# Reordering VectorE work in one retention loop and one mixer block, and rebuilding a small embedding stage, in a fused three-layer forward pass on Trainium2

## The reference, cut to what matters

```python
# first block
z   = rms_norm(x, norm1_g) @ w_in            # 18 column tiles of 128
mix = concat([gmlp(z_a), rglru(z_b), hgrn2(z_c), pool(z_d)])
x   = x + mix @ w_out
hf  = causal_dwconv(rms_norm(x, norm2_g) @ w_up)       # 2 x 2816
x   = x + (gelu(gt) * val) @ w_down
gate = sigmoid(rms_norm(x, norm3_g) @ w_pg)            # 1024 x 1024
x   = x + (p @ w_pe) * gate                            # p: 512 x 256, w_pe: 256 x 1024
x   = rms_norm(x, final_g)

# hgrn2: gated linear recurrence, 4 heads, chunks of 64;
# within a chunk the pairwise decays exp(b_t - b_s) are needed
# gmlp: vn = layer_norm(v); y = u * (lower-triangular(ws) @ vn)

# hybrid layer (twice)
o_a = sliding_window_attention(...) @ w_attn_o
o_b = rwkv7(...) @ w_rwkv_o
o_c = retention(rq, rk, rv, rg) @ w_ret_o
x   = x + (g0 * o_a + g1 * o_b + g2 * o_c) @ w_out      # g = sigmoid(gates)
x   = x + (silu(h2 @ w_ffn_gate) * (h2 @ w_ffn_up)) @ w_ffn_down

# retention, per chunk n of 128 tokens
s     = (q_n @ k_n.T) * dmat
o     = rms(s @ v_n + (q_n @ R) * xi) * silu(gate_n)
R     = R * chunk_decay + (k_n * zeta).T @ v_n
```

## Time and profile before

| | us |
|---|---|
| median of 3 runs | 2644.86 |
| the 3 runs | 2643.98, 2648.19, 2644.86 |
| profiled execution, its own time | 2648.18 |
| profiled execution, span of the trace | 2646.3 |

### The profile page before, as it was taken

One profiled execution on the slowest core, in us unless ns is written; L12 is line 12 of the kernel. 1 busy time (PEld: TensorE's weight loads), 2 busy tenths in 40 slices (PEclk: granted clock), 3 DMA queues, 4 the chain that ended last, 5 costly groups with the idle time before them and its releaser, 6 DMA issues.

```text
span 2646.3 us, 47390 instructions
## 1 busy us (share of the span) xinstructions
PE 2585.7 (98%) x16344; PEld 2020.2 (76%) x16344; DVE 1453.3 (55%) x2031; ACT 678.7 (26%) x1258; POOL 1490.1 (56%) x945
## 2 busy tenths in 40 slices
PE   8989999998999999999999999999999999999999
PEld 5768888876777677777888887777677777888887
DVE  7866555455467648764443434467648764443434
ACT  3452000034134435431200002134435531100002
POOL 4666666655544454456666666544454456566664
PEclk9999999999999999999999999999999999999999
DMA  4213332323211122223233333311122223322332
GB/s 161 67 46 112 95 94 91 93 80 108 88 57 37 48 92 64 72 73 103 89 93 95 95 95 109 95 58 37 48 92 64 72 78 97 95 91 92 95 95 95
DMA packets 72439, 222.56 MB, mean 84 GB/s; under 512 B 9312, under 2 KB 12256, under 8 KB 72288
## 3 DMA queue, kind: packets, MB, share of 16 engines
q1 hardware_dynamic: 72000, 220.46, 27.2%
q10 hardware_dynamic: 288, 0.04, 0.0%
HBM read 218.37 MB, written 2.10 MB: 83 GB/s over the span
## 4 chain that ended last, share of the span: by engine, by line
PE 90%; DVE 4%; DVEq 2%; issue 2%; DMA 1%; POOL 1%; ACT 0%; SPq 0%; ACTq 0%; POOLq 0%
PE acc L501 79%; PE bank L501 9%; DMA raw<-in_w_pg 1%; POOL w_lo L363 1%; PE bank L1098 0%; DVEq L1582 0%; DVE rw_bon L1136 0%; DVEq L1675 0%; DVE rw_SCB L1136 0%; DVE z_rw L1136 0%; DVE y_lo L1136 0%; DVE m_ta L1264 0%; DVE xg_lo L1230 0%; SPq L315 0%; DMA bs<-in_bs 0%
## 5 line engine op out<-in xcount | busy, mean ns | idle before, releaser
L363 POOL TENSOR_TENSOR w_lo<-raw,w_hi 128x1024 fp32r<-128x1024 f32 (+3 forms) x438 | 964.7, 2202 | 302.8 <-PE acc L501 274.1
L356 POOL TENSOR_SCALAR w_hi<-raw 128x1024 fp32r<-128x1024 f32 (+3 forms) x438 | 435.7, 995 | 663.5 <-PE acc L501 562.5
L501 PE MATMUL acc<-xg_hi,w_hi 128*128 128x512 f32 x2208 | 588.4, 403 | 14.0 <-issue 8.1
L501 PE MATMUL acc<-xg_lo,w_hi 128*128 128x512 f32 x2208 | 582.0, 400 | 0.0
L501 PE MATMUL acc<-xg_hi,w_lo 128*128 128x512 f32 x2208 | 580.4, 399 | 0.0
L501 PEld LDWEIGHTS acc<-xg_hi,w_hi 128*128 128x128 f32 x2208 | 408.5, 188 | 133.0 <-issue 40.2
L501 PEld LDWEIGHTS acc<-xg_lo,w_hi 128*128 128x128 f32 x2208 | 414.4, 189 | 103.1 <-issue 4.8
L501 PEld LDWEIGHTS acc<-xg_hi,w_lo 128*128 128x128 f32 x2208 | 411.4, 188 | 99.3 <-issue 0.5
L1967 ACT ACTIVATE ffn_act<-ffn_t 128x512 f32<-128x512 f32 x100 | 63.3, 633 | 775.0 <-DVEq L1196 619.5
L1136 DVE TENSOR_TENSOR x<-x,acc 128x512 f32<-128x512 f32 x104 | 71.4, 687 | 319.0 <-PE acc L501 318.5
L501 PE MATMUL acc<-hid_hi,w_hi 128*128 128x512 f32 x656 | 182.7, 396 | 3.7 <-POOL w_lo L363 1.6
(11 more groups left out here) (349 smaller groups left out, 2792.8 us busy)
## 6 DMA issues: line engine op xcount, KB each, us to landing
raw<-in_w_up SPq DMA_DIRECT2D x132, 512.0 KB, 3.6
raw<-in_w_down SPq DMA_DIRECT2D x48, 512.0 KB, 3.6
raw<-in_w_gate SPq DMA_DIRECT2D x48, 512.0 KB, 3.6
raw<-in_w_ret SPq DMA_DIRECT2D x32, 512.0 KB, 3.6
raw<-in_w_rw SPq DMA_DIRECT2D x28, 512.0 KB, 3.6
raw<-in_w_o SPq DMA_DIRECT2D x48, 256.0 KB, 2.6
raw<-in_w_in SPq DMA_DIRECT2D x18, 512.0 KB, 3.7
raw<-in_w_down SPq DMA_DIRECT2D x24, 384.0 KB, 3.0
```

What stands on the lines that cost most here:

```text
L356: nc.gpsimd.tensor_scalar(w_hi[:, s, 0:n], raw[:, s, 0:n], 1.0, 0.0, ALU.mult, ALU.add).then_inc(w_half[s], 1)
L363: nc.gpsimd.tensor_tensor(w_lo[:, s, 0:n], raw[:, s, 0:n], bits(w_hi[:, s, 0:n]), ALU.subtract).then_inc(w_split[s], 1)
L501: return nc.tensor.matmul(o, a, b, start=first, stop=last, skip_group_check=shared)
```

## The change

Four edits. (a) `take(2, 1)` of the first block moves ahead of the wait for `ea` and of the polynomial. (b) At level 3 of the hgrn2 loop `decays(4)` moves behind the three splits; at levels 1 and 2 nothing moves. (c) In the retention loop `branch(2n+1)` moves from the end of the chunk to right behind the product with the root; its own drain takes the place of the one that stood there. (d) The embedding stage: `w_pe` (1 MB) is loaded once, ahead of the first `w_up` slot, POOL splits it in four pieces behind the four last `w_down` pairs, the gate uses both slots for `w_pg` (four pairs instead of eight), and the six small matmuls of each tile go to `bank[1]` and `bank[5]` in turn, so that the accumulators hold gates alone.

```diff
-B1_IN, X_OUT, O_PAIRS, PE_PAIRS = 9, 4, 24, 8
+B1_IN, X_OUT, O_PAIRS, PE_PAIRS = 9, 4, 24, 4
 ...
+        pe_hi, _ = place("pe_hi", (2 * DC * P,), F32R, offset=scratch)
+        pe_lo, _ = place("pe_lo", (2 * DC * P,), F32R, offset=scratch + 8 * DC * P)
+        pe_raw, _ = place("pe_raw", (2 * DC * P,), offset=(at[0] + 31) // 32 * 32)
 ...
             sp.dma_start(emb[:], dram["p"]).then_inc(first_in, 16)
+            sp.dma_start(pe_raw[:], dram["w1_pe"]).then_inc(first_in, 16)
 ...
-            load(PE_PAIRS, ("w1_pg", "w1_pe"), I); I += PE_PAIRS
+            load(PE_PAIRS, ("w1_pg", "w1_pg"), I); I += PE_PAIRS
 ...
-            split(PE_PAIRS, (DC, 2), I)
+            def embedding_weights(i):
+                at = slice(i * 4 * P, (i + 1) * 4 * P)
+                pool.drain()
+                nc.gpsimd.tensor_scalar(pe_hi[:, at], pe_raw[:, at], 1.0, 0.0, ALU.mult, ALU.add)
+                pool.drain()
+                nc.gpsimd.tensor_tensor(pe_lo[:, at], pe_raw[:, at], bits(pe_hi[:, at]), ALU.subtract)
 ...
+                    for i in range(X_OUT):
+                        split_pair((n, n), I + i)
+                        embedding_weights(i)
+                I = I + X_OUT
+            split(PE_PAIRS, (DC, DC), I)
 ...
+            def embedded(j):
+                if j == 1:
+                    pe.wait_ge(root_ready, 3)
+                elif j > 1:
+                    pe.wait_ge(x_ready, 2 * DC + j - 1)
+                b = bank[(1, 5)[j % 2]]
+                for m, (w, v) in enumerate(((pe_hi, emb_hi), (pe_hi, emb_lo), (pe_lo, emb_hi))):
+                    for c in range(2):
+                        last = mm(b[:], w[:, (2 * j + c) * P:(2 * j + c + 1) * P], v[:, c, :], m == 0 and c == 0, m == 2 and c == 1)
+                last.then_inc(emb_done, 1)
+
             late(0, I, xg, full, xg_ready, 2 * DC)
             stats(3)
-            slot(1, I, em, range(2))
-            with pe.Fori(1, PE_PAIRS) as i:
-                slot(0, I + i, xg, full, early=True)
-                slot(1, I + i, em, range(2), early=True)
+            embedded(0)
+            for j in range(1, DC):
+                slot(j % 2, I + j // 2, xg, full, early=True)
+                embedded(j)
             stats(4)
 ...
             zf = z[:, 8:10, :]
-            take(2, 0, zf)
+            for s in range(2):
+                take(2, s, zf)
             dve.wait_ge(s1["ea"], 1)
 ...
             v.tensor_scalar(lp[0], lp[0], 8.0, None, ALU.mult)
-            take(2, 1, zf)
+            dve.drain()
 ...
+                if 0 < lev < 3:
+                    decays(lev + 1)
                 if 0 < lev < 4:
-                    decays(lev + 1)
                     for j in ((), (2,), (3, 0, 1))[lev - 1]:
                         splitted(y_hi[:, j, :], y_lo[:, j, :], z[:, (0, 1, 4, 5)[j], :])
                         dve.drain()
                         dve.sem_inc(y_ready, 1)
+                if lev == 3:
+                    decays(4)
 ...
             def embedding_gate(j):
-                scaled(0, I + j, ffn["t"][:]).then_inc(acc_free[0], 1)
+                scaled(j % 2, I + j // 2, ffn["t"][:]).then_inc(acc_free[j % 2], 1)
 ...
             def embedding(j):
+                b = bank[(1, 5)[j % 2]]
                 dve.wait_ge(h_act, FFC + j + 1)
-                done(1, I + j)
-                tt(bank[1][:], acc[1][:], ffn["act"][:]).then_inc(acc_free[1], 1)
+                dve.wait_ge(emb_done, j + 1)
+                tt(b[:], b[:], ffn["act"][:])
                 dve.drain()
-                tt(x[:, j, :], x[:, j, :], bank[1][:], ALU.add)
+                tt(x[:, j, :], x[:, j, :], b[:], ALU.add)
 ...
                     tt(rt["o"][:], rt["o"][:], rt["sq"][:])
-                    dve.drain()
+                    branch(2 * n + 1, O, mixed[:, 2 * n + 1, :])
                     after(s3, "silu", n)
                     tt(rt["o"][:], rt["o"][:], rt["gs"][:])
                     dve.drain()
                     splitted(tile_of(y2_hi, 0, 4, n), tile_of(y2_lo, 0, 4, n), rt["o"][:])
-                    branch(2 * n + 1, O, mixed[:, 2 * n + 1, :])
                     say(s3, "done")
 ...
-            act.wait_ge(slot_done[0], B1_PAIRS + 1)
+            act.wait_ge(slot_done[1], B1_PAIRS + 1)
```

More of the change, by code:

```diff
@@ L259, in build @@
         o_gate, o_sig = sem("o_gate"), sem("o_sig")
+        emb_done = sem("emb_done")
         load_wait = 16
@@ L455, in _ @@
             split(X_OUT, (4, 4), B1_IN + X_OUT)
-            I = ffn_split(B1_IN + 2 * X_OUT)
-            split(PE_PAIRS, (DC, 2), I)
+            def embedding_weights(i):
[4 more added lines that the diff above has]
+                nc.gpsimd.tensor_tensor(pe_lo[:, at], pe_raw[:, at], bits(pe_hi[:, at]), ALU.subtract)
+            I = B1_IN + 2 * X_OUT
+            for k, n in enumerate(PARTS):
+                split(n, (DC, DC), I); I = I + n
+                if k < len(PARTS) - 1:
+                    split(X_OUT, (n, n), I)
+                else:
+                    pool.wait_ge(first_in, load_wait * (len(FIRST) + 2))
+                    for i in range(X_OUT):
[3 more added lines that the diff above has]
+            split(PE_PAIRS, (DC, DC), I)
             with pool.Fori(0, LAYERS) as l:
@@ L1477, in _ @@
                 if k == 1:
-                    dve.wait_ge(first_in, load_wait * (len(FIRST) + 1))
+                    dve.wait_ge(first_in, load_wait * (len(FIRST) + 2))
                     for j in range(2):
@@ L1531, in low_half @@
                                        ALU.mult, ALU.subtract).then_inc(xg_ready, 1)
-            for j in range(PE_PAIRS):
+            for j in range(DC):
                 embedding_gate(j)
@@ L1957, in _ @@
                 norm_end(2 * l + 6)
-                swiglu(I, FFC + PE_PAIRS + l * FFC, 6 * DC + 2 * DC * l)
+                swiglu(I, FFC + DC + l * FFC, 6 * DC + 2 * DC * l)
                 ms(rstd_fin, 1.0)
@@ L2171, in high_half @@
                 fn(xg_hi[:, c, :], x[:, c, :], ACT.Identity, scale=K["gains"][:, G_L, c:c + 1]).then_inc(hi_ready, 1)
-            for j in range(PE_PAIRS):
+            for j in range(DC):
                 act.wait_ge(h_pre, FFC + j + 1)
                 fn(ffn["act"][:], ffn["t"][:], ACT.Sigmoid).then_inc(h_act, 1)
-                if j < PE_PAIRS - 1:
+                if j < DC - 1:
                     finished(j)
             act.drain()
-            act.wait_ge(slot_done[0], B1_PAIRS + 1)
+            act.wait_ge(slot_done[1], B1_PAIRS + 1)
             for c in range(2):
@@ L2406, in _ @@
                 roots(2 * l + 6, False)
-                gates(FFC, FFC + PE_PAIRS + l * FFC, ACT.Silu, SILU)
+                gates(FFC, FFC + DC + l * FFC, ACT.Silu, SILU)
                 high_halves(4 * DC + 2 * DC * l, G_L + 2 + 2 * l)
@@ L2463, in lay_out @@
     ffn("w1", f["w_up"], f["w_down"])
-    d["w1_pg"] = slots(f["w_pg"]).reshape(DC, P, DC * P)
-    d["w1_pe"] = slots(f["w_pe"]).reshape(DC, P, 2 * P)
+    d["w1_pg"] = slots(f["w_pg"])
+    d["w1_pe"] = np.ascontiguousarray(slots(f["w_pe"]).reshape(DC, P, 2 * P).transpose(1, 0, 2)).reshape(P, 2 * DC * P)
     conv = f["ffn_conv_w"].reshape(3, 2, FFC, P).transpose(3, 2, 1, 0).reshape(P, -1)
```

## The result

Before 2646.96 us (median of 7 runs, 2643.98 to 2652.08), after 2652.79 us (7 runs, 2649.46 to 2659.61). The ratio is 1.0024, with a 95% interval of 1.0014 to 1.0033: slower by some 6 us, where 2637.8, that is 7.1 faster, was forecast. The profiled execution took 2655.4, span 2653.4, PE busy 98% as before.

What follows compares the result with a forecast made beforehand. PE, busy 98%, bounds the kernel; only its idle and slow time can be won. Terms -7.5 + 0.5 - 0.9 + 1.6 - 0.8 = -7.1 gave 2637.8 us on the median, own range 2634 to 2641, whole range 2632 to 2651.

Steps and rivals of the forecast that it cites:

- four such places: Retention, chunks 1 and 2 of both layers: POOL may get ahead of DVE, PE idling 2.0 each; forecast counted none.
- rivals 2 and 3: Retention, all four places caught: at full clock +8.2, 2646.0, chance 0.12; with lowered clock 14.6, 2652.4, chance 0.11.
- rival 3: Retention: all four places caught, each idle lowering the clock; 4 x (2.05 + 1.6) = 14.6, 2652.4; chance 0.11.
- 1036.53 for the difference: Retention, chunks 1 and 2: predicted start of the difference into `y_lo`, a tie with POOL's `w_lo` at 1036.54.
- the first tie: Retention, chunks 1 and 2: silu product predicted to start at 34.6, level with POOL's `w_hi` at 1034.60.
- The prediction's own sign for the latter: Retention: PSUM-reading `rt_kz<-bank` took 0.68 while `w_lo` may still be running.
- Chunk 0: Retention, between chunks 0 and 1: PE's 2.95 wait for `acc[1]` becomes about 3.0 for `rt_kz`; -0.4 per layer.
- +0.5 forecast: First `w_up` slot: cost of the 1 MB `w_pe` transfer queued ahead of it; bounds 0 and +4.
- POOL's wait of 1.75 did not show as a wait of PE: First `w_up` slot, at 208.74: PE taken to have at least some lead over POOL's transfer wait.
- The stage itself: Embedding stage: PE runs its slots at full rate, gaining 6.1, and the tail wins 1.4; sum -7.5.
- is then spent at the next place at which PE waits for DVE: Edit a, first block: PE's lead goes into a longer wait at 93.05; -0.9 kept, bounds -3.3 and +0.7.
- +1.6 forecast: Edit b, level 3: PE starts 1.4 earlier, ACT's unbroken work 4.0 later; bounds -1.4 and +3.5.

Runs made afterwards that it cites:

- only_c: The kernel before with edit c alone: 1.0047 of its time, 2660.29 against 2646.67 us.
- c_mid: The kernel before with the retention eviction between the silu product and the split, one product later than in edit c: 0.9997 of its time.
- only_d: The kernel before with edit d alone: 0.9996 of its time, 2645.26 against 2646.67 us.
- d_late: The kernel before with edit d alone, its 1 MB transfer behind the first eight `w_up` pairs: 0.9983 of its time, 2642.24 against 2647.24 us.
- b_d: The kernel before with edits b and d: 1.0001 of its time.
- after_no_b: The changed kernel with edit b undone: 1.0016 of the time of the kernel before.
- c_pieces: The kernel before with edit c and POOL's conversions for 24 output pairs per layer cut into 256-column pieces: 1.0057 of its time, 2660.77 us.

## Why the prediction was wrong

**Edit c: the step that failed.** "There are four such places (two chunks, two layers). In the forecast none is caught." That put at nothing a term which rivals 2 and 3 price at 8.2 and 14.6. All four were caught, and in only_c and in the changed kernel without edit b too: twelve of twelve, with `y_lo` at 2.70 to 2.91. So it wasn't the bad luck of one tie. The prediction's 1036.53 for the difference holds only if DVE wins the first tie and holds `w_hi` up; where it did (1034.63 in only_c) the difference came 0.01 to 0.02 behind `w_lo`. Where `w_hi` led the silu product, by 0.01, the difference came 0.2 behind. Neither way was free. Alone edit c measured 13.6, where rival 3 (all four, each with slow matmuls, given 0.11) comes to 13.8, its 14.6 less the 0.8 at chunk 0. The prediction had the mechanism, the place and the price, and then took two ties for the good side.

That rival 3's 2652.4 is within 0.4 of the measured 2652.8 is luck. In the changed kernel edit c cost 7, edit a won 3.4 more than forecast, and the transfer cost some 3 more; these misses cancel in part, and the two numbers start from medians of before that are 2.1 apart.

By the rule of the Trainium skill ("SBUF — State Buffer", section "SBUF: two separate sides") that was cited, the port pair is held exclusively for a whole instruction. The traces agree: 2.71 and 2.91 for a 0.69 product behind `w_lo`, and 0.69 for the PSUM-reading eviction beside `w_hi` in c_mid, at 1033.45. The prediction's own sign for the latter was misread: its `rt_kz` at 1039.58 came after `w_lo` had ended, at 1038.93. The kernel before does show it, in the eviction at 1036.61, which took 0.68 beside that `w_lo`. Chunk 0 came out as argued: a wait moved from `acc` to `rt_kz`, -0.4 forecast in each layer, +0.6 in only_c. In layer 1 of the changed kernel it was 3.2 ahead there, since after its idle of 2.45, at 1007.16, no slow stretch followed, and since the kernel before ran slowly at that place; in layer 2 it was 0.5 ahead.

**Edit d: the transfer.** +0.5 forecast; 3.4 between only_d and d_late in the ratios. In the six traces that have the transfer early PE loses 1.5 (b_d) to 5.7 (after_no_b) at the first w_up slot, and 3.7 in the changed kernel's; the three that have it late lose nothing. "POOL's wait of 1.75 did not show as a wait of PE" gave it hidden lead that wasn't there: in these six POOL's wait rose by 2.1 to 3.3, PE idled 1.2 to 2.7, and in the changed kernel slow matmuls behind the idle made up the rest. In four of the five traces in which PE arrives there 3 to 4 early it loses 3.7 to 5.7, in the fifth 1.7; b_d had no such lead and lost 1.5. So a part of the larger losses may be lead that was spent; no run tells the two apart. The upper bound of 4 held for the medians, not for every trace. The stage itself was sized well: slots of 6.98 without idle, PE idle 5.54 for 7.11 in the tail, its two `xg_lo` products 1.41 for 3.45 in the row below; 7.7 in the trace against 7.5.

```profile
643.60 1.41 DVE L1572 SCALAR_TENSOR_TENSOR xg_lo<-x,gains,xg_hi 128x512 fp32r<-128x512 f32 x2
```

POOL's four pieces for `w_pe` cost nothing, as forecast.

**Edit a:** -0.9 forecast, -4.3 measured. The step by which PE's lead "is then spent at the next place at which PE waits for DVE" failed: the wait there kept its length. Rows at 90.59 and 87.11 show 1.35 and 1.42.

**Edit b:** +1.6 forecast, +1.7 measured (with an interval that holds 0, so the agreement says little). ACT was late as was said: it starts at 139.03, 2.15 behind PE's first matmul, where it was 4.06 ahead, and PE waits at two later levels.

```profile
139.03 2.19 ACT L2008 ACTIVATE m_tf<-m_tf 128x1024 f32<-128x1024 f32 x2 [14.10 <-DVEq L1366]
```

**The sum.** Forecast -7.1; with the measured parts (a -4.3, b +1.7, c +7 in place, d -1.4) it is +3.0, and the whole measured +5.8; with the 13.6 that edit c costs alone it would be +9.6. What lies between is what stays open above. The range of 2632 to 2651 held all four lost ties at a full clock (2646.0) and ended short of the same with slow matmuls (2652.4).

## What to carry to other kernels

A stall on a shared resource is decided by who comes first, so a product moved by 0.6 us can cost 2 at each turn; where the sum of durations puts two starts within a tenth of each other, plan for losing, and ask what the other outcome does to the next tie. Move a PSUM-reading operation under the other engine's hold, not ahead of the SBUF-only operations that then fall behind it. A transfer put ahead of another that is already waited for makes it later: here POOL's wait for the transfer behind 1 MB grew by 2.1 to 3.3 us. And one trace against one trace names a place, but its price needs several.

## What the runs showed of the hardware

DVE, when it waits for POOL, takes its turn between two of POOL's instructions: with `w_lo` cut in four pieces the 0.69 difference took 1.08 in c_pieces. But a piece costs more than its share: 128x256 took 0.70 a piece, against 2.39 / 4 = 0.60 as a quarter of one instruction.

POOL is held up by DVE too: `w_hi` took 1.60 in place of 1.05 where the silu product was first, at 1034.63 in only_c. And a small instruction is held as well as a large one: 2.17 in place of 0.17 for 128x2 values, at 58.19 in the kernel before.

After an idle of 1.94 that ended at 1032.11 the granted clock was 0.57 of full over 1033 to 1037 in the changed kernel. After the same 1.94, at 1042.73 in only_c, it was 1.00 over 1042 to 1047, and after 2.45, at 1007.16 in the changed kernel, 1.00 over 1007 to 1010. After 1.73, at 1067.08 in only_c, the first eight matmuls of 128x128 still took the full rate's 1.13, and over 1068 to 1072 the clock was 0.57. The length of the idle alone did not decide it in these runs, and it is what the prediction's price for an idle went by.
